# Recurrence of a hybrid decoder layer: b and k loaded straight into their expanded buffers by sixteen transfers per chunk

## The reference, cut to what matters

```python
sa = jnp.einsum('bhvk,bhk->bhv', state, a_t)
state = state * w_t[:, :, None, :] + sa[..., None] * b_t[:, :, None, :] + v_t[..., None] * k_t[:, :, None, :]
y_t = jnp.einsum('bhvk,bhk->bhv', state, r_t)
```

## Time and profile before

| | |
|---|---|
| time, median of 3 runs | 2601.85 us (2597.11 to 2603.88) |
| the profiled execution's own time | 2603.83 us |
| its span, first to last instruction | 2601.9 us |
| busy: PE / PEld / DVE / ACT / POOL | 94% / 76% / 62% / 45% / 18% of the span |
| mean granted TensorE clock | 0.973 |
| DMA packets, all / under 512 bytes | 488076 / 72396 |
| phase_recur | about 570 to 888 us |

### The profile page before, as it was taken

The page is one execution under the profiler, slowest core; times in us unless marked ns, Lnnn a source line. Parts: engine busy times, 40 slices in busy tenths (PEclk is TensorE's granted clock), DMA queues, the critical chain, the costliest instruction groups (busy, mean ns, idle before and its releaser), DMA issues. The chain is left out here.

```text
span 2601.9 us, 43203 instructions
## 1 busy us (share of the span) xinstructions
PE 2447.2 (94%) x16932; PEld 1988.2 (76%) x16932; DVE 1612.1 (62%) x1925; ACT 1170.7 (45%) x1823; POOL 479.0 (18%) x396
## 2 busy tenths in 40 slices
PE   6999999968999599979999999999999999999997
PEld 4777767647888488768888878888878888788886
DVE  2766797945865454456666666666676666666666
ACT  4656564523444345444444444444534444444443
POOL 4646464532333434300000000000000000000000
PEclk9999999988999799989999999999999999999999
DMA  6373735345676357853333543334443334333322
GB/s 175 96 227 113 227 122 187 122 162 137 168 185 158 103 180 227 263 180 97 97 97 97 194 125 92 92 94 143 148 129 93 92 92 158 114 97 97 97 81 81
DMA packets 488076, 353.98 MB, mean 136 GB/s; under 512 B 72396, under 2 KB 438396, under 8 KB 487420
## 3 DMA queue, kind: packets, MB, share of 16 engines
q1 hardware_dynamic: 429116, 293.24, 37.9%
q10 hardware_dynamic: 58816, 58.73, 6.8%
HBM read 272.21 MB, written 79.69 MB: 135 GB/s over the span
## 5 line engine op out<-in xcount | busy, mean ns | idle before, releaser
L2250 DVE TENSOR_TENSOR p_acc<-late_bank,p_acc 128x512 f32<-128x512 f32 x320 | 221.1, 691 | 194.9 <-PE late_bank L125 184.2
L123 PE MATMUL late_bank<-p_dn_hi,p_a_hi 128*128 128x512 f32 x704 | 282.1, 401 | 18.0 <-DVE p_acc L2247 12.6
L2220 DVE SCALAR_TENSOR_TENSOR p_cv<-p_ub,p_cpar,p_cv 128x512 f32<-128x512 f32 x176 | 127.6, 746 | 252.5 <-ACT p_cv L2135 252.5
L124 PE MATMUL late_bank<-p_dn_lo,p_a_hi 128*128 128x512 f32 x704 | 281.6, 400 | 0.0
L125 PE MATMUL late_bank<-p_dn_hi,p_a_lo 128*128 128x512 f32 x704 | 281.3, 400 | 0.0
L123 PE MATMUL p_ppr<-p_hT_hi,p_w_hi 128*128 128x512 f32 x576 | 234.8, 408 | 0.4 <-DVE p_hT_lo L670 0.2
L397 POOL TENSOR_TENSOR p_w_lo<-p_w_raw,p_w_hi 128x1024 fp32r<-128x1024 f32 x72 | 184.7, 2565 | 239.4 <-ACT p_w_hi L465 239.4
L124 PE MATMUL p_ppr<-p_hT_lo,p_w_hi 128*128 128x512 f32 x576 | 227.5, 395 | 0.0
L125 PE MATMUL p_ppr<-p_hT_hi,p_w_lo 128*128 128x512 f32 x576 | 227.2, 394 | 0.0
L2124 ACT ACTIVATE p_ub<-late_bank 128x1024 f32<-128x1024 f32 x88 | 90.3, 1026 | 272.1 <-PE late_bank L125 265.7
L2146 ACT ACTIVATE p_a_hi<-p_cv 128x512 fp32r<-128x512 f32 x88 | 55.6, 632 | 339.0 <-DVE p_cv L2230 339.0
(11 more groups left out here) (256 smaller groups left out, 5710.2 us busy)
## 6 DMA issues: line engine op xcount, KB each, us to landing
first_up_raw<-in_w_up SPq DMA_DIRECT2D x176, 512.0 KB, 5.0
p_dn_raw<-in_w_down SPq DMA_DIRECT2D x88, 512.0 KB, 4.2
p_w_raw<-in_w_in SPq DMA_DIRECT2D x72, 512.0 KB, 3.9
x_block<-in_x SPq DMA_DIRECT2D x8, 1024.0 KB, 6.7
p_x<-in_x SPq DMA_DIRECT2D x16, 512.0 KB, 5.1
scratch_x<-p_x ACTq DMA_DIRECT2D x16, 512.0 KB, 2.8
scratch_h_hi<-p_h_hi ACTq DMA_DIRECT2D x16, 512.0 KB, 5.8
scratch_h_lo<-p_h_lo ACTq DMA_DIRECT2D x16, 512.0 KB, 4.5
```

Of the source, the lines that this page charges most:

```text
L123: nc.tensor.matmul(out, lhs_hi, rhs_hi, start=start, stop=False)
L124: nc.tensor.matmul(out, lhs_hi, rhs_lo, start=False, stop=False)
L2220: nc.vector.scalar_tensor_tensor(cv[s][:, i, :], ub[s][:, i, 1:1 + TB], cpar[s][:, i, 1:2], cv[s][:, i, :], ALU.mult, ALU.add).then_inc(s_ ...
L2250: nc.vector.tensor_tensor(dst, bank[:, 4 + n % 4, :], dst, ALU.add).then_inc(s_acc, 1)
```

## The change

The two loads of `bt` and `kt` into compact tiles, the compact tiles and the eight POOL copies go. In their place SP writes `bk[p]` directly from the scratch tensors, with sixteen transfers per chunk: for each parity, for b and k, for each half of the partitions, and for each of the two blocks of that parity. One transfer moves 64 partitions x 4 pairs x 32 tokens, 32 KB in 256 pieces of 128 bytes. SP waits before them for `bk3` of iteration i-1, which POOL waited for before. PE waits for the sixteen transfers in the place of POOL's eight copies.

```diff
                         else:
-                            sp.wait_ge(s_bk, ONE + n * 8)
-                            for dst, key in ((bt, "bt"), (kt, "kt")):
-                                sp.dma_start(dst[:, :, :], scr[key][:, :, tok]).then_inc(s_in, 16)
+                            if n == 1:
+                                sp.wait_ge(s_const, ONE + 1)
+                            else:
+                                wait_full(sp, i - 1, "bk3")
+                            for e in range(2):
+                                for kind, key in ((e, "bt"), (1 - e, "kt")):
+                                    for h2 in range(2):
+                                        off, rows = 64 * kind + 32 * h2, slice(64 * h2, 64 * h2 + 64)
+                                        for c in range(e, CH, 2):
+                                            sp.dma_start(bk[p][rows, :, c, off:off + C], scr[key][rows, :, bass.ds(n * SC + c * C, C)]).then_inc(s_bk, 16)
...
-                    if a1:
-                        n = i + 2
-                        gp.wait_ge(s_in, ONE + n * 32 + 32)
-                        if b:
-                            wait_full(gp, i - 1, "bk3")
-                        if i > 3:
-                            gp.wait_ge(s_mo, ONE + i - 3)
-                        if n == 0:
-
-                            gp.sem_inc(s_bk, 8)
-                        for e in range(2 if n else 0):
-                            for kind, src in ((e, bt), (1 - e, kt)):
-                                for h2 in range(2):
-                                    off = 64 * kind + 32 * h2
-                                    nc.gpsimd.tensor_copy(
...
                     if d:
-                        gp.wait_ge(s_bk, ONE + 8 * min(i + 3, N))
                         gp.wait_ge(s_in2, ONE + (i - 2) * 32)
...
                         if j == 0:
-                            pe.wait_ge(s_bk, ONE + i * 8 + 24)
+                            if i > -2:
+                                pe.wait_ge(s_bk, ONE + (i + 2) * 256)
```

More of the change, by code:

```diff
@@ L988, in phase_recur @@
         ar = [scr["first_ar"]] + [sb(f"ar{i}", [P, 2, PAIRS, SC]) for i in range(1, BATCH)]
-        bt = scr["first_bt"]
-        kt = scr["first_kt"]
         bonus = sb("bonus", [P, PAIRS, SC])
@@ L1025, in phase_recur @@
         s_const = sem("zeros_written")
-        s_in = sem("b_k_loaded")
         s_arl = [sem(f"a_r{i}_loaded") for i in range(2)]
         s_in2 = sem("bonus_gate_loaded")
-        s_bk = sem("bk_built")
+        s_bk = sem("bk_loaded")
         s_gram = sem("gram_done")
@@ L1164, in body @@
                         if n == 0:
-                            sp.sem_inc(s_in, 32)
                             sp.sem_inc(s_arl[0], 32)
@@ L1242, in body @@
                     a1, a2, b, o, c, d = stages(i)
-                    if a1:
-                        n = i + 2
-                        gp.wait_ge(s_in, ONE + n * 32 + 32)
-                        if b:
-                            wait_full(gp, i - 1, "bk3")
-                        if i > 3:
-                            gp.wait_ge(s_mo, ONE + i - 3)
-                        if n == 0:
-                            gp.sem_inc(s_bk, 8)
-                        for e in range(2 if n else 0):
-                            for kind, src in ((e, bt), (1 - e, kt)):
-                                for h2 in range(2):
-                                    off = 64 * kind + 32 * h2
-                                    nc.gpsimd.tensor_copy(
-                                        by_parity(bk[p][64 * h2:64 * h2 + 64, :, :, off:off + C], e),
-                                        by_parity(src[64 * h2:64 * h2 + 64, :, :].rearrange("p j (c t) -> p j c t", t=C), e)
-                                    ).then_inc(s_bk, 1)
                     if d:
-                        gp.wait_ge(s_bk, ONE + 8 * min(i + 3, N))
                         gp.wait_ge(s_in2, ONE + (i - 2) * 32)
```

## The result

The changed kernel takes 2710.74 us (median of 4 runs, 2708.65 to 2715.76), the kernel before 2602.41 us in the runs beside it: ratio 1.0424 [1.0407, 1.0441], **108 us slower**. The forecast was 59 us slower, 2661 us, with a range to 2693 us. The direction came out as forecast, and SP became the bound as forecast; the size did not, and the time lies outside the range.

The account below looks back on a forecast made before the run. PE's order of work was taken to bound the recurrence, with SP then becoming the bound: start 6.5 us later, thirteen iterations of 20.7 us, 17 us to the last grams, +59 us, 2661 us; eight in ten, 2634 to 2693 us.

Parts of the forecast that it names:

- SP became the bound: In the recurrence, SP's iteration grows from 14.7 to 20.7 us against PE's 16.2; chance 0.87.
- The wait for `bk3`: SP's new wait ahead of the sixteen loads, for `bk3` of iteration i-1: cost 0, with 19.6 us of room.
- The chain of `mo`: In iteration 13, from gate's landing through POOL, ACT's store and write of `mo` to the grams: 17 us.
- this path: In iteration 13, sixteen issues, then `at` and `rt` issued and landed, before the grams: 13.5 us, the shorter way.
- the price of one issue: Each new transfer on SP costs 0.488 us, taken from xt; sixteen cost 7.8 us an iteration.
- the upper bound: One new issue on SP at 0.67 us, by bt's length and a gap; with no relief 24 us an iteration, 2704 us.
- The relief: Part of the stretching of SP's single issues goes with fewer large transfers ahead: 0.5 us off an iteration.
- The tail: After the last grams, the last serial iterations and next phases keep their length; the lower clock adds 2 us at most.
- the spare time: What SP can take on in an iteration before it bounds: 1.4 us to spare beside its 14.7 us of issuing.
- Hidden: Rival: SP's new issues fit in its spare time and only the start is 6.5 us later: 2608 us; chance 0.06.
- faster: Rival: without POOL's copies PE's pauses go, at most 15.9 us, giving 2586 us; chance 0.03.
- Clogged: Rival: the 4096 small packets a chunk delay all transfers behind them; period 26 us, +130 us, 2730 us; chance 0.04.

Follow-up runs that it names:

- experiment 1: The changed kernel with the same sixteen transfers a chunk issued by POOL in place of SP: 2609.61 us, ratio 1.0007 to the kernel before.
- experiment 6: The changed kernel with two 256 KB loads straight into `bk`, in wrong places, for the sixteen transfers, and no POOL copies: 2600.52 us, ratio 0.9979 to the kernel before.
- experiment 2: The changed kernel with each of the sixteen transfers cut to one pair of heads of four, 64 pieces: 2708.14 us, ratio 1.039 to the kernel before.
- experiment 5: The changed kernel with all of b and k in eight transfers a chunk, 512 pieces each: 2645.44 us, ratio 1.0153 to the kernel before.
- experiment 7: The changed kernel with pairs of chunks loading `bk` in different forms (partitions, pieces, source); run once for issue durations, everything about 0.6 us.
- half_count: The changed kernel with only the eight transfers of `bt` a chunk, `kt` left out: 2637.31 us, ratio 1.0116 to the kernel before.
- experiment 8: The changed kernel with an unused fifth pair in scratch `bt` and `kt`, and varied transfer forms; run once: 32 partitions 432 ns, 128 partitions 508, 64 partitions 617.

## Why the prediction was right in kind and wrong in size

**What it had right.** SP becomes the bound: it issues without a break (its timeline after), and moving the same issues to POOL takes the loss back (experiment 1). The wait for `bk3` is free: 0.3 us. The data are no bound: DMA share 0.49, and with a quarter of the bytes 102 of 108 us remain. POOL's copies lay beside other work: counted as 0, worth 5 us (experiment 6), 479.0 to 430.4 us of POOL's busy time. The chain of `mo` is there: POOL waits for the gate, ACT for POOL, and PE for ACT. The timeline of POOL, ACT and PE, after, in iteration 12, and at the last chunk's grams and behind them:

```profile
904.45 1.26 POOL L1250 TENSOR_TENSOR p_mo<-p_mo,p_bonus 128x512 f32<-128x512 f32 x1 [21.21 <-DMA p_gate<-scratch_g]
...
907.09 0.39 ACTq L1289 DMA_DIRECT2D scratch_mix<-p_mo  x1
907.53 0.60 ACT L1270 ACTIVATE p_bkt<-p_bank 128x512 f32<-128x512 f32 x1 [7.10 <-POOL p_mo L1252]
908.18 1.11 PE L1514 MATMUL p_bank<-p_ident,p_bk 128*128 128x128 f32 x4 [5.18 <-ACT p_bkt L1270]
...
937.90 0.69 PE L1526 MATMUL p_bank<-p_ar,p_bk 128*64 128x64 f32 x16 [1.12 <-issue]
...
951.82 1.11 PE L1514 MATMUL p_bank<-p_ident,p_bk 128*128 128x128 f32 x4 [4.62 <-ACT p_bkt L1270]
```

POOL stands 21.21 us for the gate, the last transfer in SP's order; ACT stands 7.10 us behind POOL, and PE's transposes 5.18 us behind ACT. PE names ACT, ACT names POOL, POOL names the transfer: three rows that follow one late issue to the engine that pays.

**Right by luck.** The last grams run at 937.90 us, 16.8 us after the start of iteration 13, and the forecast had 17, by the chain of `mo`. But they waited for `rt`. Its row in the list of transfers (last number: us from issue to landing), and its issue in SP's timeline:

```profile
p_ar<-scratch_rt SPq DMA_DIRECT2D x1, 256.0 KB, 4.0
...
933.85 0.63 SPq L1185 DMA_DIRECT2D p_ar<-scratch_rt  x1
```

Issued at 933.85 us, it landed at 937.82 us, and the grams began 0.08 us later, after 1.12 us for which the profile names no releaser. In eight of the fourteen iterations from 0 to 13 (0 to 5, 8 and 13) the first grams begin less than 0.1 us after `rt` has landed; in the other six they begin 1.1 to 2.9 us after it. The forecast gave this path 13.5 us, with sixteen issues at 0.488 us; at their true price it took 16.7 us, by chance the length of the other chain.

**Where the 53 us went.** The span of the profiled execution grew by 112.1 us (the medians by 108), the forecast's sum by 58.9. By its terms:

| term | forecast | measured |
|---|---|---|
| SP's start of the recurrence (585.87 against 581.14) | 0 | +4.7 |
| iteration -1 (611.78 - 585.87 = 25.9 against 16.5) | +6.5 | +9.4 |
| iterations 0 to 12 | 13 x 20.7: +59.3 | 13 x 23.8: +99.6 |
| start of iteration 13 to the last grams | -6.9 | -7.1 |
| after the last grams | 0 | +5.5 |
| sum | +58.9 | +112.1 |

**The step that failed is the price of one issue**, "I take 0.488 us, by xt, which has the same count and size of pieces". It measured 0.707 us with its gap: 16 x 0.707 = 11.3 us in place of 7.8, which is 3.5 us in each of thirteen iterations and in iteration -1. The kind of reason was wrong, and not only the number: an issue on SP depends little on the count of pieces (64, 256, 512 pieces: 597, 612, 649 ns in the median, experiments 2 and 5) and not on their size (128 and 256 bytes: 612 ns, experiment 7). The row of `bt`, 630 ns, was the nearer one, because its source is the very tensor that the new transfers read; it was in the text as the upper bound, worked out as 24 us an iteration and 2704 us, and then left outside the range. The relief that the forecast took off, 0.5 us, was 1.1 us (the four uv alone went from 2.78 to 2.07 us an iteration in the mean), so the sum is 14.7 - 1.3 + 11.3 - 1.1 = 23.6 us, by the timeline 23.5 and 0.3 of waits. That the new issues get stretched too was named as a risk and is in the 0.707.

The reason given for the relief was wrong as well. The forecast had single issues stretched by large transfers ahead of them. In the thirteen iterations SP has 38 issues of over 0.75 us before and 40 after: they are about as many, only 16 of the 40 now fall on the new transfers. They go with another thing, the packets of the queue "instruction" (before, then after):

```profile
q8 instruction: 38, 0.62, 1.3%
...
q8 instruction: 39, 0.64, 0.9%
```

After, 39 of the 40 long issues overlap in time with such a packet of 16 KB, and each of these ends 0.36 to 0.50 us after the packet does; before it is 33 of 38, and the other five packets came while SP issued nothing long. So the stretched issues seem to be pauses for instructions, some 2.6 to 3 us an iteration in both kernels, that land on whatever SP is issuing. No run changed this, so it is seen and not shown.

**The smaller terms.** Iteration -1 is the same price again. The 4.7 us at the start lie ahead of the change: over the profiled executions of the kernels of this study, which share the first phase, the recurrence's first POOL work starts anywhere from 568.7 to 577.6 us, so such a difference between two profiles is not read. The tail is a miss: "what comes after keeps its length" and "2 us at most at the end" for the clock. From the last grams to the next phase it is 7.4 us longer (5.5 us to the end of the span), of which 4.62 us are PE's wait behind ACT at 951.82 us, the chain of `mo` once more, after the last load. The lower clock is there as forecast, 0.83 in the middle against 0.98, and seems to be paid inside PE's pauses.

The forecast was also of two minds on the spare time: it took 16.1 us an iteration for the 1.4 us that SP has to spare, and 17.1 us where it asks what an issue may cost to be hidden. Over the thirteen iterations SP's period was 16.1 us and PE's 16.8 us. It changes neither the sum nor the verdict on the rivals.

**The rivals.** Hidden and faster: it needed under 0.23 us an issue, or 0.38; no new issue median in any kernel was under 0.43. Clogged: refuted by experiments 2 and 5, although the result lies nearer to its 2730 us than to the forecast. The Trainium skill says ("DMA: Bandwidth & Descriptors", "Issuing engines are not separate DMA queues") that several issuing engines save only the time to initiate, usually small beside the transfer. Experiment 1 agrees with its first half: issued by POOL, the transfers cost SP nothing. Its second half is the one that misleads here: a new issue takes 0.61 us where the landing of the same transfer takes 2.6 us (half_count), but sixteen issues in a row on one busy engine were worth over 100 us.

## What to carry to other kernels

Where an engine issues transfers back to back, count its issues as work: number times price, against its spare time for an iteration. Here the spare was 3.4 to 3.7 us, five transfers, and sixteen moved the bound; putting the data of two transfers into one cost 0.12 us on SP in the mean and saved 0.7, while on POOL it saved nothing. Take the price of an issue from a transfer with the same tensors and the same partitions, not from one with the same number of pieces; where two rows compete, the range has to hold both. And if a run is to hold something constant, look in its profile that it did: in experiment 1 the packets changed.

## What the runs showed of the hardware

- An issue on SP took 0.43 to 0.45 us in the median for xt, atm and uv, all on 32 partitions, and 0.60 to 0.65 us for every form of the direct loads (experiments 2, 5 and 7). An unused fifth pair in each partition's row of the tensor in HBM took 0.17 us off an issue on 32 partitions (to 0.43 us), 0.13 us off one on 128 (to 0.51 us), and nothing off one on 64 (experiment 8). Why is open.
- POOL issues 256 pieces in 0.615 us, as fast as SP, and 512 pieces in 1.35 to 1.77 us, where SP takes 0.649 us. Its transfers appear as packets of 1 KB (7,680 for 240 transfers), SP's as packets of 128 bytes.
- After, 39 of SP's 40 long issues overlapped a 16 KB packet of the instruction queue and ended 0.36 to 0.50 us after it.
- With PE busy for 235.97 of 309.32 us, in pauses of a few microseconds, the granted clock fell from 0.98 to 0.83; PE's busy time an iteration rose from 16.18 to 18.93 us for about the same matmuls, and, as is argued here and was not run by itself, cost nothing while SP was later.
